# Eight places fewer for one-element results: most of a kernel's tensors start 32 bytes lower

## The reference

```
h = einsum("cd,chkd->chk", xc, u_sel)
a = gelu(h, approximate=False) * gc
y = einsum("chk,chkd->cd", a, v_sel)
```

## Time and profile before

| | us |
|---|---|
| median of 3 runs | 3206.47 (3203.27 to 3208.0) |
| the profiled execution | 3206.9 |
| its span, first to last instruction | 3205.1 |
| TensorE busy | 3106.4 (97%) |
| VectorE busy | 1866.1 (58%) |
| ScalarE busy | 1624.9 (51%) |
| GpSimd busy | 675.3 (21%) |

### The profile page before, as it was taken

One profiled execution on the slowest core, in us unless ns is written; L12 is line 12 of the kernel. 1 busy time (PEld: TensorE's weight loads), 2 busy tenths in 40 slices (PEclk: granted clock), 3 DMA queues, 4 the chain that ended last, 5 costly groups with the idle time before them and its releaser, 6 DMA issues.

```text
span 3205.1 us, 63948 instructions
## 1 busy us (share of the span) xinstructions
PE 3106.4 (97%) x25426; PEld 3023.9 (94%) x25426; DVE 1866.1 (58%) x3255; ACT 1624.9 (51%) x2600; POOL 675.3 (21%) x292
## 2 busy tenths in 40 slices
PE   8999998999999999889999999999999999999999
PEld 8999998999999898768999999999999999999999
DVE  5545555645444357756677788644447865554444
ACT  5666765466677642365444443444444444444443
POOL 3333332444434342203444310000000000000000
PEclk9999998999999899999999999999999999999999
DMA  5433433444433354324455544455554455555554
GB/s 194 139 137 131 144 131 111 167 171 169 146 132 133 113 183 149 111 79 145 162 181 183 173 147 142 170 184 184 183 184 165 152 174 184 183 182 183 183 183 157
DMA packets 72287, 506.59 MB, mean 158 GB/s; under 512 B 7904, under 2 KB 10592, under 8 KB 11232
## 3 DMA queue, kind: packets, MB, share of 16 engines
q1 hardware_dynamic: 71584, 503.09, 45.3%
q10 hardware_dynamic: 576, 1.72, 0.2%
HBM read 502.69 MB, written 2.10 MB: 157 GB/s over the span
## 4 chain that ended last, share of the span: by engine, by line
PE 90%; DVE 5%; ACT 3%; issue 2%; DMA 0%; DVEq 0%; SPq 0%; ACTq 0%
PE bank L448 13%; PE bank L450 12%; PE bank L449 12%; PE bank L2150 4%; PE bank L2151 4%; PE bank L2152 4%; PE banks L2151 4%; PE banks L2150 4%; PE banks L2152 4%; PE bank L462 3%; PE banks L1945 3%; PE banks L1946 3%; PE bank L1946 3%; PE bank L1945 3%; PE banks L1947 3%; PE bank L1947 3%
## 5 line engine op out<-in xcount | busy, mean ns | idle before, releaser
L425 ACT ACTIVATE whi<-raw 128x1024 fp32r<-128x1024 f32 x898 | 940.9, 1057 | 1059.4 <-PE bank L450 446.8
L432 DVE TENSOR_TENSOR wlo<-raw,whi 128x1024 fp32r<-128x1024 f32 x667 | 811.5, 1228 | 477.9 <-ACT whi L425 476.9
L432 POOL TENSOR_TENSOR wlo<-raw,whi 128x1024 fp32r<-128x1024 f32 x231 | 614.7, 2661 | 1079.6 <-ACT whi L425 1074.0
L448 PE MATMUL bank<-xa_hi,whi 128*128 128x272 f32 (+1 forms) x2048 | 604.8, 295 | 2.9 <-DVE wlo L432 1.8
L450 PE MATMUL bank<-xa_hi,wlo 128*128 128x272 f32 (+1 forms) x2048 | 596.9, 291 | 0.0
L449 PE MATMUL bank<-xa_lo,whi 128*128 128x272 f32 (+1 forms) x2048 | 595.2, 291 | 0.0
L448 PEld LDWEIGHTS bank<-xa_hi,whi 128*128 128x128 f32 x2048 | 394.9, 193 | 7.6 <-issue 2.7
L449 PEld LDWEIGHTS bank<-xa_lo,whi 128*128 128x128 f32 x2048 | 396.3, 193 | 0.7
L450 PEld LDWEIGHTS bank<-xa_hi,wlo 128*128 128x128 f32 x2048 | 393.8, 192 | 0.0
L448 PE MATMUL bank<-xb_hi,whi 128*128 128x256 f32 (+1 forms) x1152 | 332.4, 289 | 6.5 <-DVE f_qg L999 6.1
L450 PE MATMUL bank<-xb_hi,wlo 128*128 128x256 f32 (+1 forms) x1152 | 327.9, 285 | 0.0
(11 more groups left out here) (417 smaller groups left out, 6684.6 us busy)
## 6 DMA issues: line engine op xcount, KB each, us to landing
raw<-in_w SPq DMA_DIRECT2D x251, 1024.0 KB, 4.8
raw<-in_v SPq DMA_DIRECT2D x128, 1024.0 KB, 5.3
raw<-in_u SPq DMA_DIRECT2D x96, 1024.0 KB, 4.8
hT<-in_hT SPq DMA_DIRECT2D x4, 544.0 KB, 8.6
out<-hT SPq DMA_DIRECT2D x8, 256.0 KB, 3.2
r_keys<-in_keys ACTq DMA_DIRECT2D x1, 1024.0 KB, 5.0
c_mask<-in_masks ACTq DMA_DIRECT2D x1, 320.0 KB, 2.9
params<-in_params SPq DMA_DIRECT2D x1, 238.5 KB, 2.6
```

Of the source, the lines that this page charges most:

```text
L425: act.activation(whi[:, (2 * t.q + half) % 4, :], raw[:, t.q, half * 1024:(half + 1) * 1024], ACT.Copy).then_inc(w_hi_done, 1)
L432: eng.tensor_tensor(wlo[:, t.q, at], raw[:, t.q, at], whi[:, slot, :].bitcast(F32), ALU.subtract).then_inc(w_lo_done[half], 1)
L448: te.matmul(ps, hi, x[0][:, kk, cols], start=(kk == 0), stop=False)
```

## The change

`token` gets 24 places in place of 32. `table_for` takes its places from ScalarE's eight, from the same counter as `lone`. The number and order of instructions stay as they are.

```diff
-        token = tensor(ctx, "token", [P, 32])
+        token = tensor(ctx, "token", [P, 24])
...
-        tables_asked = [0]
-
         def table_for(act, function):
 
-            tables_asked[0] = (tables_asked[0] + 1) % 8
-            k = 24 + tables_asked[0]
+            token_at[act] = (token_at[act] + 1) % 8
+            k = 8 * list(token_at).index(act) + token_at[act]
             act.activation(token[:, k:k + 1], con("one"), function)
```

## The result

The kernel after takes 3183.9 us (median of 4 runs, 3178.57 to 3186.95), the kernel before 3205.55 us (4 runs beside them, 3203.27 to 3208.0). The ratio is 0.9936 with a 95% interval of 0.9924 to 0.9947: faster by 21.7 us, 0.6%. I had forecast 3206.5 us and no difference.

The account below looks back on a forecast made before the run. TensorE's matmul pace was taken to bound the kernel, with other streams hidden behind it. All terms were taken as 0, so the forecast was the median of the runs, 3206.5 us, no difference (70%), range 3196 to 3217 us.

Parts of the forecast that it names:

- What bounds the kernel: Whole span: TensorE, busy 97%, sets the time by its start-to-start matmul cost; the other streams are hidden behind it.
- The shared places: One-element results of `table_for` and `lone` on ScalarE: sharing places costs 0, at most 0.2 us showing.
- VectorE, ScalarE and GpSimd: Their work on moved tensors: cost 0; bounds 3.3 us either way on VectorE, 2.9 us upwards on ScalarE; GpSimd's split hidden.
- The transfers: `hT` loads at the start and stores at the end: cost 0, with 1.2 us either way.
- TensorE's own reads: The 21,504 matmuls with split operands: moved starts taken as 0, with 7.6 us up or down.
- the 0.36 ns between two stages: Down projection at 118.9 ns a matmul against up projection at 119.3; taken as the price of a place, 7.6 us on 21,504.
- the row that I leaned on: Two-pass float matmuls over 272 columns, lines 922 and 667: medians 392 and 393 ns; said not to settle split reads.
- TensorE's pace falls: Rival, hot loops: most operands now start on a multiple of 64, so matmuls get faster; 7.6 us, 3198.9 us, chance 7%.
- the excess is the same in stages with one and with four distances: Argument against a faster pace: down and up projections exceed the 2.4 GHz need alike, within 0.36 ns.
- The pace rises: Rival, matmul triples: mixing operands on and off a multiple of 64 slows TensorE; 0.36 ns, 7.6 us, 3214.1 us, chance 8%.
- The clock: Rival, first layer: half-clock drops fall elsewhere; all gone 3196.5 us, twice as many 3216.5; chance 7% fewer, 8% more.
- up to 9.7 ns a matmul at stake: Skill page gives 109.2 ns at 256 columns, rows 118.9; if operands' starts caused the gap, up to 209 us at stake.

Follow-up runs that it names:

- the twins with thinned traffic: Kernels before and after, each with most down-projection loads and splits cut to 8 columns of each half; one run each, 3201.17 and 3183.93 us.
- rest only: Kernel before with 224 bytes of padding behind `whi`, so `whi` stays and everything behind it is 224 bytes higher; 3192.09 us, ratio 0.9965.

## Why the prediction was wrong

**What bounds the kernel** was right: TensorE's pace, and no wait took part. **The shared places** cost nothing, as forecast. **VectorE, ScalarE and GpSimd** kept their medians within 3 ns. **The transfers** were right as far as can be seen: `hT` lands 0.8 us earlier, inside the 1.2 us that I allowed and inside its own scatter of 7.3 to 8.6 us.

**TensorE's own reads** is the step that failed. I put this term at 0, with 7.6 us either way; measured, it is a gain of about 20 us (20.9 by the windows, 18.9 by the spans behind the first layer). It had two faults. First, the price. I took the 0.36 ns between two stages for what a place can be worth. But both stages ran in one layout. The pace is not a sum of prices of single places; it belongs to the whole triple of matmuls with all its distances. Measured, the same two stages differ by 1.26 and 1.06 ns between before and after, a third by 2.8, and over all layouts the up products go from 1677 to 1717, 2.8 ns. That operands' places can set the pace was in my list, but at nothing in the sum; the size was off by a factor of three to eight. Second, the row that I leaned on: two-pass matmuls with a start on and off a multiple of 64, both 392 ns. It was true and answered another question. The kernel with everything 32 bytes higher shows that starts are worth nothing; a start and a distance are different things, and no row of before had two distances with the same work.

**The rivals.** "TensorE's pace falls" came true, at 7% and 3198.9 us where 3183.9 was measured. What I held against it, "the excess is the same in stages with one and with four distances", is the comparison that misled me. Its reason, starts on a multiple of 64, was wrong as well. That the time fell at all is no credit to that rival's reasoning. "The pace rises" has a case too, only elsewhere: with 128 bytes upwards the down projection does 1669. Its picture, weights and moving operand placed differently to each other, was nearer to what the runs show, with the sign wrong for this step. The clock gave some of the difference between the profiled spans, and the difference of 21.7 us between the medians doesn't need it.

By the Trainium skill's page on TensorE (TensorE: Matmul & The Clock Gate, section "Wait — 56ns, not 53.3ns?"), an estimate put up to 9.7 ns a matmul at stake. The part that distances were seen to decide is 2.8 ns in the up products. No layout here came below 116 ns at 256 columns, and no run shows what the remaining 7 ns are. The rule of the Trainium skill's page SBUF — State Buffer (section "Who interferes with whom"), that TensorE never waits on another engine for SBUF, is borne out by the twins with thinned traffic: 1681 and 1700 matmuls as with full traffic, within one. I had drawn too much from it: that others don't disturb TensorE doesn't mean that it can't disturb itself. The Trainium skill's page TensorE: Matmul & The Clock Gate calls TensorE's two read ports independent (section "Step-by-step: what each phase is for"). Measured, moving `coef_hi` alone by 32 bytes changes the pace by 1.1%, and moving all operands together by 32 bytes doesn't; so the place of one read relative to the other matters, whatever the ports are.

**What stays open.** Which pairs of reads meet, and when. The period of 256 bytes was tested in one direction and two stages; no rule in the distances fits all fifteen rows above. Two layouts ran one stage at two paces, so a row of the table need not be all that its layout can do. That a collision of the two reads makes the delay is the reading that is left after the other engines were excluded, in the down projection, and not shown directly.

## What to carry to other kernels

When TensorE alternates between loading weights and streaming a moving operand without gaps, try a few paddings of 32 bytes between the weights' buffers and the operands: a line each, up to 1.2% here, and no row of one layout predicts it. Judge them by the number of matmuls in a window without gaps. In the layouts before and after it repeated within one in 1700, but in two others the second of two like stages ran at another pace than the first, so look at every stage, and at several executions. Change one tensor at a time, as stages have their own best distance. And any edit that changes the size of a small tensor moves all behind it: before its gain is put down to what the edit meant, run the same edit with the size padded back.

## What was not expected of the hardware

One layout can run a stage at two paces, and keeps the one that it falls into for as long as the windows reach. In the kernel that is 32 bytes higher behind `token`, the first down projection has 1690 matmuls in 200 us and the second, with the same operands, 1701. In the one in which all behind `whi` moved ("rest only"), it is 1701 in the first and 1669 in the second: in steps of 50 us, 427 six times from 2100 us on, and 419 six times from 2850 us on. The kernel that is 224 bytes higher has 425 in 50 us in the output projection at 1110 us, and in the one at 1480 us 431, which after has in both; the kernel that is 480 bytes higher has 425 in both.

```profile
1480.00:1530.00 50.00, 50.00 (x431) 50.00 (x430) 39.69 (x36) 27.13 (x54) 24.13 (x9) 1.00 0.54 189
1110.00:1160.00 50.00, 50.00 (x425) 50.00 (x424) 31.83 (x28) 26.32 (x54) 23.04 (x10) 1.00 0.53 182
```

So the two streams may lock into one of several rhythms; no run shows what picks one. It would fit the scatter of the layout 32 bytes higher, 3165.4 to 3179.6 us over its four runs, and of "rest only", 3187.1 to 3197.1 over five, against 3203.3 to 3208.0 of the kernel before. Of each only one execution was profiled: of the first the slowest, of the second the fastest.
